# Where the expert gathers stand in the GpSimd program: all three at once, or one ahead of each scatter

## What is computed

```python
eid = g_sel[:, None] * EXPERTS_PER_GROUP + top_i        # 2 of 32 experts for each of 1024 tokens
...
xs = h2[slot_tok].reshape(n_blocks, MOE_BLOCK, d)
def expert_block(args):
    xb, e = args
    return (jax.nn.silu(xb @ w_gate[e]) * (xb @ w_up[e])) @ w_down[e]
...
return jnp.zeros((n, d), h2.dtype).at[slot_tok].add(ys)
```

## Time and profile before

| | |
|---|---|
| median of 3 runs | 1266.11 us (1264.2 to 1266.54) |
| the profiled execution's own time | 1268.91 us |
| its span | 1267.1 us |
| TensorE busy in the span | 1197.3 us, 94% |
| VectorE, ScalarE, GpSimd busy | 552.2, 279.5, 261.4 us |
| the experts' matmuls, first and last | 653.3 us and 1221.7 us from the span's start |
| granted TensorE clock, mean | 0.988 |

### The profile page before, as it was taken

The page is one execution under the profiler, slowest core; times in us unless marked ns, Lnnn a source line. Parts: engine busy times, 40 slices in busy tenths (PEclk is TensorE's granted clock), DMA queues, the critical chain, the costliest instruction groups (busy, mean ns, idle before and its releaser), DMA issues. The chain is left out here.

```text
span 1267.1 us, 31527 instructions
## 1 busy us (share of the span) xinstructions
PE 1197.3 (94%) x13908; PEld 943.3 (74%) x13908; DVE 552.2 (44%) x1043; ACT 279.5 (22%) x561; POOL 261.4 (21%) x330
## 2 busy tenths in 40 slices
PE   5899999999999999999979999999999999999997
PEld 1799888888788887888756776767776776766873
DVE  1756553432578888666842222222122222222227
ACT  3832212111556665422200000000000000000003
POOL 0000000001100000100043335343443524332220
PEclk9899999999999999999989999999999999999998
DMA  9648844435566775421469999999999999999628
GB/s 379 251 180 301 291 137 142 170 121 170 189 224 174 165 177 136 160 100 51 157 239 414 416 413 414 411 408 390 384 385 378 400 381 373 390 385 364 263 73 348
DMA packets 96844, 345.33 MB, mean 273 GB/s; under 512 B 18483, under 2 KB 47011, under 8 KB 69059
## 3 DMA queue, kind: packets, MB, share of 16 engines
q1 hardware_dynamic: 75795, 312.04, 66.4%
q10 hardware_dynamic: 11696, 14.44, 3.9%
q0 software_dynamic: 9216, 16.82, 3.6%
HBM read 310.18 MB, written 35.14 MB: 273 GB/s over the span
## 5 line engine op out<-in xcount | busy, mean ns | idle before, releaser
L2255 PE MATMUL p_layers<-slot,xt 128*32 128x256 f32 x3744 | 238.2, 380 | 14.7 <-issue 10.3
L2255 PEld LDWEIGHTS p_layers<-slot,xt 128*32 128x32 f32 x3744 | 168.7, 110 | 76.6 <-issue 46.7
L2204 DVE TENSOR_TENSOR arena<-arena,p_layers 128x384 f32<-128x384 f32 x32 | 17.7, 554 | 329.1 <-ACT arena L2182 329.1
L2137 POOL DMA_INDIRECT y_rows<-arena x96 | 95.7, 997 | 309.2 <-DVE arena L2221 288.4
L2182 ACT ACTIVATE arena<-p_layers 128x384 f32<-128x384 f32 x32 | 15.7, 491 | 546.7 <-PE p_layers L2255 546.7
L2270 PE MATMUL p_layers<-slot,ht 128*32 128x256 f32 x2016 | 118.2, 379 | 1.4 <-issue 1.4
L2255 PE MATMUL p_layers<-raw,xt 128*32 128x256 f32 x1632 | 108.3, 385 | 7.4 <-issue 5.1
L2270 PEld LDWEIGHTS p_layers<-slot,ht 128*32 128x32 f32 x2016 | 91.9, 110 | 20.8 <-issue 1.9
L1896 POOL DMA_INDIRECT arena<-h_rows,arena x96 | 98.4, 1025 | 40.2 <-issue 28.6
L2072 PE MATMUL p_a<-tokens_high,half_high 128*128 128x512 f32 (+1 forms) x272 | 101.7, 374 | 0.2 <-DVE half_low L705 0.2
L2255 PEld LDWEIGHTS p_layers<-raw,xt 128*32 128x32 f32 x1632 | 71.4, 111 | 40.4 <-issue 23.8
(11 more groups left out here) (388 smaller groups left out, 2038.1 us busy)
## 6 DMA issues: line engine op xcount, KB each, us to landing
slot<-in_w_down SPq DMA_DIRECT2D x42, 1024.0 KB
slot<-in_w_gate SPq DMA_DIRECT2D x39, 1024.0 KB
slot<-in_w_up SPq DMA_DIRECT2D x39, 1024.0 KB
raw<-in_w_ada SPq DMA_DIRECT2D x24, 1024.0 KB, 7.5
raw<-in_w_gate SPq DMA_DIRECT2D x17, 1024.0 KB
raw<-in_w_up SPq DMA_DIRECT2D x17, 1024.0 KB
raw<-in_w_down SPq DMA_DIRECT2D x14, 1024.0 KB
x<-qk_rows SPq DMA_DIRECT2D x6, 1664.0 KB, 8.5
```

The source lines that it names most:

```text
L2137: pool.indirect_dma_start(y_slices, bass.IndirectOffsetOnAxis(ap=s.row[:, b, n:n + 1], axis=0), x.y[n % 2][:, b * SLICE:(b + 1) * SLICE], ...
L2255: last = pe.matmul(gate_up[quad(g), b, :, :], x.xt[n % 2][:, k, b, :], weights[:, :, r, g * ES:(g + 1) * ES], start=(k == 0), stop=(k == K ...
```

## The change

GpSimd's program alone is changed. gather() now issues one block's gather, and its callers loop over the blocks, so the first gathers, of experts 0, 1 and 2, are issued as before (those of expert 2 in iteration 0). From iteration 1 on the gathers of expert n + 2 no longer stand at the head of the iteration. After the table work GpSimd waits until first_layer(n) is done (`used` at `used_by(n, 1)`); then, for each block b, it issues the gather of block b of expert n + 2, waits for `y_ok` of block b of expert n - 1, and issues that block's scatter. The wait for turn_x(n) stays at the head.

```diff
+                for b in range(BLOCKS):
+                    gather(pool, a, s, 0, b)
...
-def gather(pool, a, s, n):
+def gather(pool, a, s, n, b):
...
-            def scatter(n):
+            def scatter(n, ahead=None):
 
                 for b in range(BLOCKS):
+                    if ahead is not None and ahead < NE:
+                        gather(pool, a, s, ahead, b)
                     pool.wait_ge(y_ok, BLOCKS * n + b + 1)
                     pool.indirect_dma_start(y_slices, ...
...
             for n in range(NE):
                 if n + 2 < NE:
                     pool.wait_ge(x_turned, n + 1)
-                    gather(pool, a, s, n + 2)
+                if n == 0:
+                    for b in range(BLOCKS):
+                        gather(pool, a, s, 2, b)
...
                 if n >= 1:
-                    scatter(n - 1)
+                    pool.wait_ge(used, used_by(n, 1))
+                    scatter(n - 1, n + 2)
             scatter(NE - 1)
```

More of the change, by code:

```diff
@@ L1448, in _ @@
                 pool.wait_ge(listed_ok, 3)
-                gather(pool, a, s, 0)
+                for b in range(BLOCKS):
+                    gather(pool, a, s, 0, b)
                 pool.wait_ge(coded, 4)
@@ L1889, in keep_part @@
     return s.keep[:, first:first + n]
-def gather(pool, a, s, n):
+def gather(pool, a, s, n, b):
     slices = a.h_rows.rearrange("n (g d) -> (n g) d", g=GROUPS)
-    for b in range(BLOCKS):
-        pool.indirect_dma_start(s.xg[n % 2][:, b * SLICE:(b + 1) * SLICE], None, slices, bass.IndirectOffsetOnAxis(ap=s.token[:, b, n:n + 1], axis=0),
-                                bounds_check=GROUPS * N - 1, oob_is_err=False).then_inc(s.gathered[n % 2], 16)
+    pool.indirect_dma_start(s.xg[n % 2][:, b * SLICE:(b + 1) * SLICE], None, slices, bass.IndirectOffsetOnAxis(ap=s.token[:, b, n:n + 1], axis=0),
+                            bounds_check=GROUPS * N - 1, oob_is_err=False).then_inc(s.gathered[n % 2], 16)
 def list_rows(dve, c, digits, rowf, wrap, token, row):
@@ L2141, in _ @@
             steps = Counter(pool, over_ready)
-            gather(pool, a, s, 1)
+            for b in range(BLOCKS):
+                gather(pool, a, s, 1, b)
             for n in range(NE):
```

## The result

The changed kernel takes 1301.26 us, median of four runs (1298.74 to 1307.16); the kernel before takes 1265.92 us on the same chip (four runs, 1264.2 to 1266.54). The ratio is 1.0288 [1.0251, 1.0325]: 2.9% slower. The direction is the one predicted. The number was 1288 us, and the measured time lies 5 us above the upper end of the predicted range, 1296 us. The profiled execution took 1300.37 us, with a span of 1298.5 us, 31.5 us more than that of before.

The account below looks back on a forecast made before the run. TensorE was held bound by droughts, stretches without instructions while GpSimd makes descriptors back to back for over 2.5 us. 1268.91 + 22 = 1291 us profiled, less 2.8 us gives 1288; own range 1282 to 1294, overall 1228 to 1296.

Parts of the forecast that it names:

- The bound: TensorE in the first layer runs out of instructions while GpSimd makes gather and scatter descriptors; 2.25 us lost per expert.
- The run of five: On GpSimd, scatter, gather, scatter, gather, scatter follow with 0.3 us gaps, 845.4 to 851.6 us; chance 0.50, 1288 us.
- Its length: Back-to-back descriptor making on GpSimd lasts 6.6 to 7.0 us against 5.77; 1.1 us longer taken (0.85 to 1.25).
- the tail: TensorE's starvation outlasts the last DMA on GpSimd by 0.8 us behind a gather, 0.4 to 0.8 behind a scatter.
- The price: Each us of descriptor making beyond 2.5 us costs TensorE 0.7 us; 0.77 us per expert, 22 us for 29.
- The costs of nothing: Around the first layer, holding scatters back and gathers arriving later cost 0; table work 0, at most 1 us in one or two iterations.
- The added wait: `used` holds GpSimd's three scatters behind the first layer; cost 0, covered by some 30 us.
- The later landing: Third gather's rows arrive at 855.0, turn_x starts 6.4 us later on VectorE; slack 3.8 us, cost 0.
- Only gathers: Rival: gathers but not scatters starve TensorE, so the change is faster; 0.28, of which 0.18 near 1233, 0.10 near 1218.
- the supply has barely more than TensorE uses: Rival: TensorE's instruction reserve refills slowly, total descriptor making counts, so no change, 1266 us; chance 0.17.
- Cooling: Rival: longer starvation drops TensorE's clock, 1.6 us more per expert, 46 us, 1334 us; chance 0.05.
- The first rival: If starvation vanishes, weight and row DMAs at 413 GB/s at most limit the gain: 1211 to 1226 us; 0.10 near 1218.

Follow-up runs that it names:

- e3: Kernel before, with a pause of 2.2 us on GpSimd ahead of each expert's first gather only: 1235.86 us, ratio 0.9756.
- e5: Kernel before, with each gather behind a pause and an expert's three scatters held until the third y, then issued together: 1248.45 us, ratio 0.9854.
- e1: Changed kernel without the added wait for the first layer (`used`) ahead of the gathers and scatters: 1321.08 us, ratio 1.0437 to the kernel before.
- e9: Changed kernel with one small memset (a gap of about 1.1 us) ahead of gathers 1 and 2: 1228.95 us, ratio 0.9739 to the kernel before.
- e7: Kernel before, with one small memset (a gap of about 1.1 us) ahead of each gather: 1228.55 us, ratio 0.9745.
- e6: Changed kernel with a pause of 2.2 us (four small memsets) ahead of gathers 1 and 2: 1271.82 us, ratio 1.0102 to the kernel before.
- e2: Kernel before, with a pause of 2.2 us on GpSimd ahead of each of an expert's three gathers: 1227.76 us, ratio 0.9690.
- e4: Kernel before, with gathers spread by TensorE's progress through the first layer and one pause ahead of gather 1, scatters as before: 1227.92 us, ratio 0.9752.
- e11: Kernel before, with gathers of experts 2 to 31 fetching 64 of 128 partitions: 1264.19 us, ratio 1.0020.
- e10: Kernel before, with gathers of experts 2 to 31 as direct GpSimd DMAs of fixed rows of the same size: 1234.76 us, ratio 0.9787.

## Why the prediction was right, and where it wasn't

**The bound, right.** TensorE's supply of instructions, starved by descriptor making on GpSimd; e3 and e5 show that it takes gathers and scatters alike.

**The run of five, right.** Gather 0 alone, then scatter, gather, scatter, gather, scatter at steps of 1.31 and 1.33 us, 5.30 us from the first start to the last where 5.2 were worked out.

**Its length, the step that failed.** The run was to be 1.1 us longer than that of before, 0.85 to 1.25 at the bounds; the window grew by 1.56 us (3.2 to 4.76). Of the 0.46 us missed, 0.1 is the earlier start (+2.47 for +2.57), 0.1 the steps, and 0.26 the tail, the time from the end of the last DMA's row to the end of the drought: "behind a scatter no row shows one, so 0.4 to 0.8 us". From the start of the last scatter to the drought's end I had taken 1.67 us and the regular groups show 1.93, a tail of 0.9. The 0.8 was read well, behind a run of four; what had no ground was to take it as the most that a run of five could have. The table shows in its place that the tail grows with the run, whether a gather or a scatter stands last: 0.6 to 0.7 us behind three DMAs, 0.8 to 0.9 behind four, 0.9 behind five, 1.0 behind six. A fifth DMA moves the end by 1.45 us, from +5.77 to +7.22.

**The price, right.** 18.90 - 15.54 = 3.36 us lost in a window of 4.76 us is 0.71 per us. With 1.11 us in place of 0.77 the 29 experts cost 32 us in place of 22, and the profiled execution 1300.4 us in place of 1291. The other 4 us between 1288 and the median come from how executions differ: I had taken off 2.8 us since the profiled execution of before stood above its median, and that of the changed kernel stands 0.9 us below it.

**The costs of nothing, right, with less room than it seems.** The added wait costs nothing (e1: without it the time rises; e9 has it and is as fast as e7, which hasn't). The later landing costs nothing: the third gather starts at 839.28 and VectorE turns the rows at

```profile
844.96 1.60 DVE L2202 STREAM_TRANSPOSE xt<-arena 128x768 f32<-128x768 f32 x1 [4.83 <-DMA arena<-h_rows,arena]
```

5.7 us later, as predicted, and no weight load waits for it. e6 shows the cover gone: with the third gather 3.8 us later, all of the slack that had been worked out at 17.79 us an expert, TensorE waited 44 us from 700 to 1200 us.

**The rivals.** "Only gathers" fell with e5, "the supply has barely more than TensorE uses" with e3 and e7, where the same descriptors in pieces cost next to nothing. Cooling didn't come: the first layer's matmuls behind droughts of 4.8 us still take 380 ns in the mean, and the changed kernel's granted clock stays at 1.00 in all of its experts from 700 us on. It isn't far off, though. In e1 the clock fell once among the experts, right behind a drought of 4.7 us (1074.8 to 1079.5), no longer than those of the changed kernel: from 1079.6 to 1083.1 us 36 matmuls ran at a granted clock of 0.51. In e6 it fell three times, behind waits for turned rows of 2.5, 3.1 and 6.2 us. The prediction misread the clock in that rival: the 1.00 of the earlier trace rows belongs to the stretch ahead of the slow matmuls, and from 659.0 to 662.2 us, where they ran at 634 ns, the granted clock is 0.53, the lower of the two levels. The first rival's view that the DMAs can't follow a TensorE without droughts did hold, for other kernels: 1211 to 1226 us were worked out, and e2, e4, e7 and e9 reach 1228 to 1229.

**What stays open.** Which shared thing GpSimd's indirect DMAs take from TensorE's instruction supply, and what the reserve of 2.5 us is: no run here changed anything there. One rival can be read off the trace. Instructions come in packets of 16 KB on a queue of their own, q8, 62 of them from 700 to 1190 us in the kernel before, in which 7940 matmuls ran, one packet for 128 pairs. In 12 of 26 droughts no such packet is under way, and those under way in one take 0.89 to 1.09 us, those outside 0.89 to 1.20: packets that come late don't explain the droughts. Open too: whether the time of a run counts or the number of its DMAs, whether direct DMAs do the same, and whether the weights' 413 GB/s can be raised, which now bounds the best versions.

## What to carry to other kernels

If TensorE shows short "issue" gaps at regular distances, look at what GpSimd does in the 2.5 us before them: indirect DMAs issued back to back for longer than that starve it, and in this kernel each us of drought costs 0.7. Keep such runs to two, and put 1.1 us of something else between them (here a small memset); total time on GpSimd and its share of the span say nothing about it. And when a stretch is spaced out, count again the slack of what is delivered last in it: a pause of 2.2 us in place of 1.1 gave back everything that was gained.

## What was not expected of the hardware

- A small gap refills the whole reserve: 0.85 us behind a lone scatter (e11) and 1.1 us behind a pair (e9) are enough. 0.3 us are not, 0.54 to 0.62 us behind a run of four are not (e1), and a gap of 0.62 us within a drought doesn't end it.
- The reserve is the same for every kind of run, 2.48 to 2.63 us in the means of the table. The Trainium skill (Advanced Engine Details and Errata, Engine Queue Depths) has 64 instructions in TensorE's queue, "complicated with tiling", by which the estimate was 1.7 us at two instructions a pair; the runs show some 0.8 us more.
- An indirect DMA costs GpSimd nearly the same for half the rows (0.96 for 1.03 us), a direct one of the same 128 KB 0.59 us in the mean (e10).
- Leaving out half of each gather's rows gained nothing (1.0020 [1.0007, 1.0032]), two idle instructions an expert in the changed kernel brought its ratio to the kernel before from 1.0288 to 0.9739.
